# VectorE adds a tile to x before it makes the preceding tile's low part: the order of two loops in a two-layer encoder trunk

## The chip, the core and the metric

The kernel runs on one core of one Trainium2 chip. The metric is the device time of one execution in microseconds (us), the median of several runs. The engines are named as the profile names them: PE (TensorE, matrix products), PEld (its weight loads), DVE (VectorE), ACT (ScalarE), POOL (GpSimd) and SP (SyncE, which issues most transfers here).

## What is computed

Two layers of an encoder over 1088 tokens (1024 of a new stream, 64 of a running one) with 1024 channels; float32 throughout:

```python
hn = rmsnorm(x, g_mix)
proj = hn @ w_in
y_a, h_last = s5_mixer(u_a, ...)
y_b, new_hist = pool_mixer(u_b, ...)
x = x + jnp.concatenate([y_a, y_b], axis=-1) @ w_out
hf = rmsnorm(x, g_ffn)
x = x + jnp.square(jax.nn.relu(hf @ w_ff1)) @ w_ff2
```

`rmsnorm` divides by the root of the mean square over the channels and multiplies by a gain. After the second layer a last `rmsnorm` gives the output.

## The kernel before

x lies in SBUF with channels on the partitions, as `KD` = 8 tiles of 128 channels x 1088 tokens. Each product of float32 matrices is made of three products of fp32r parts: a number is split into a high part (a rounding copy, made by ACT) and a low part (the number minus the high part, made by DVE), and PE computes high x high, low x high and high x low. One output tile of 128 channels x 1088 tokens fills three banks of PSUM; there are two such tiles (`ps`), used in turn by the tile's number. A tile with `k` input tiles takes 9 `k` matmuls (three products, three column ranges): 36 in the products with four input tiles, 72 in those with eight.

The weights come in blocks of 128 x 1024 through two slots: SP fetches a block (`w_raw`), ACT makes its high part (`split_hi`, L861, tile `w_high`), DVE its low part (`split_lo`, L1223, tile `w_low`). A block serves two output tiles of four input tiles, or one of eight. SP fetches block b when the low part of block b-2 is made, since that frees the slot.

The stages of a layer, in order: `WIN` (u = normalised x times w_in), the two mixers with the first residual products (`WOB`), the gate (`GLU`), the **second residual products** (`WOA`: x += W_out y_a, 8 tiles of four input tiles), then the feed-forward in `NC` = 8 chunks. A chunk `cc` has `KA` = 4 tiles of the first matrix (`ff1_tile`, eight input tiles each) and 8 tiles of the second (`ff2_tile`, four input tiles each), which are added to x. After the last chunk of layer 0 comes layer 1's `WIN`. There the norm is begun as soon as x is final, tile by tile: the input of the next products is x times gain, in two parts, tiles `h_high` and `h_low`; the division by the root mean square is put on the result of those products later, once the sum of squares is known (`rms`).

Two loops over the 8 output tiles m thus end with making h: that of the second residual products in both layers, and that of the last chunk of layer 0's feed-forward. All engines work their own queue in the order in which the program was written; semaphores join them. For each tile m:

- PE computes tile m into `ps[m % 2]`. It waits in `tile_at` for `tile_free`, that is, until DVE has taken tile m-2 out of the same PSUM tile.
- DVE `add_to_x` (L1548, two instructions) adds the PSUM tile to x[m] and so frees it.
- ACT `finish` (L885, L887) then makes the square of x[m] (tiles `work_r` and `work_s` in turn, `rms` for m = 0) and `h_high`[m]; after an odd m, `ahead` makes the high part of the next weight block (L861). At the end of layer 0's feed-forward ACT also issues a transfer that keeps x[m] in DRAM.
- POOL `add_squares` (L1764) adds the square to `rms`.
- DVE, after an odd m, makes the low part of that weight block, `split_lo` (L1223).
- DVE `low_h` (L1227) waits for `h_high`[m] and makes `h_low`[m].

In `products` (L509 is the matmul) the first tile of the following stage takes its eight input tiles one after the other and waits before input tile k for `h_low`[k] (`h_made`). After that tile PE sums the squares over the channels (`sum_part`, L538), which waits for POOL's last addition; ACT takes the root (L895), DVE the reciprocal (`inverse`, L1239), and only then does DVE take the first output tile out of PSUM (L1682 or L1501).

Of the kernel before, what the change touches and what calls it, by code (L numbers as in the profile page):

```python
# [14 lines left out]
LAYERS = 2  # L15
# [7 lines left out]
KD = DM // P  # L23
# [10 lines left out]
B_WIN, B_WOB, B_GLU, B_WOA, B_FF = 0, 8, 12, 14, 18  # L34
FFC = DFF // P // KD
NC = 2 * FFC
# [15 lines left out]
L_FFN, L_NEXT, L_SCALE, NLP = 0, 8, 16, 20  # L52
# [62 lines left out]
def hybrid_trunk(nc, x_in, w_blocks, w_pool, prep_in, gain0, layer_in, dstate_in,  # L115
# [10 lines left out]
    with ExitStack() as ctx:  # L126
# [3 lines left out]
        def at(name, offset, shape, dt=F32):  # L130
            assert offset + int(np.prod(shape[1:])) <= words, name
            return nc.alloc_sbuf_tensor_at(name, list(shape), dt, offset=base + 4 * offset)
# [109 lines left out]
        lp = at("layer_params", S + 136, [P, NLP])  # L242
# [87 lines left out]
        def f32(ap):  # L330
            return ap.bitcast(F32)

        def halves(tile, flat, also=()):

            yield (tile[:, 0:2, 0:WIDE], flat[:, 0:2 * WIDE].rearrange("p (c n) -> p c n", c=2),
                   *(a[:, 0:2 * WIDE].rearrange("p (c n) -> p c n", c=2) for a in also))
            yield (tile[:, 2, 0:2 * J], flat[:, 2 * WIDE:T], *(a[:, 2 * WIDE:T] for a in also))
# [15 lines left out]
        def ff1_tile(l, cc, m):  # L353
            return l * NT + T_FF + 12 * cc + m

        def ff2_tile(l, cc, m):
            return l * NT + T_FF + 12 * cc + KA + m

        def ff_block(l, cc, n):

            return l * NB + B_FF + 8 * cc + n

        def w_parts(b):

            hi, lo = (whi_last, wlo_last) if b >= LAYERS * NB - 2 else (whi, wlo)
            return hi[:, b % 2, :], lo[:, b % 2, :]

        def last_tile(i):

            c, m = divmod(i, KD)  # L370
            a, b = CHUNKS[c]
            return c, m, slice(a * J, b * J), ps[i % 6 // 3][:, i % 3, 0:(b - a) * J]
# [832 lines left out]
        def _(v):  # L1205
# [13 lines left out]
            def split_lo(b):  # L1219
                if b < LAYERS * NB:  # L1220
                    v.wait_ge(whi_made, b + 1)
                    hi, lo = w_parts(b)
                    v.tensor_tensor(lo, raw[:, b % 2, :], f32(hi), ALU.subtract).then_inc(wlo_made, 1)  # L1223

            def low_h(m, n, gain):
                v.wait_ge(hhi_made, n + 1)
                v.scalar_tensor_tensor(hlo[:, m, :], x[:, m, :], gain[:, m:m + 1], f32(hhi[:, m, :]),  # L1227
                                       ALU.mult, ALU.subtract).then_inc(h_made, 1)
# [99 lines left out]
            def rotations(l, piece, tmp=None):  # L1328
                d = prep_of[l]
                tmp = d.rot_tmp if tmp is None else tmp  # L1330
                if piece == 0:
                    first_rotations(step, copy, tt, l, (1, 2, 4, 8), tmp)
                elif piece == 1:
                    if l == 0:
                        v.wait_ge(first_rot, 1)
                    for n in (16, 32):
                        doubled(step, tt, l, n, slice(0, 2), tmp)
                else:
                    h = piece - 2
                    doubled(step, tt, l, 64, h, tmp)  # L1340
                    step.wait()
                    for i in range(2):
                        ins = v.tensor_copy(d.rot[:, h, i, :, JP:J], d.rot[:, h, i, :, 0:JS])
                        if i:
                            ins.then_inc(rot_made, 1)
                        else:
                            step(ins)
# [144 lines left out]
            for l in range(LAYERS):  # L1492
                LB, LT = l * NB, l * NT
# [51 lines left out]
                def add_to_x(n, m):  # L1545
                    v.wait_ge(tile_done, n + 1)
                    for pt_, xt in halves(ps[n % 2], x[:, m, :]):
                        ins = v.tensor_tensor(xt, pt_, xt, ALU.add)  # L1548
                    ins.then_inc(tile_free, 1)
# [119 lines left out]
                    v.tensor_tensor(yal[:, m, :], ya[:, m, :], f32(yah[:, m, :]), ALU.subtract).then_inc(ya_made, 1)  # L1669
                for m in range(KD):  # L1670
                    add_to_x(LT + T_WOA + m, m)
                    if m % 2:
                        split_lo(LB + B_WOA + m // 2 + 2)
                    low_h(m, l * 16 + 8 + m, lp[:, L_FFN:L_FFN + KD])

                inverse(2 * l + 1)
                for cc in range(NC):
                    for m in range(KA):
                        n = ff1_tile(l, cc, m)
                        v.wait_ge(tile_done, n + 1)  # L1680
                        for pt_, out, r in halves(ps[n % 2], tr[:, :], (rms[:, :],)):
                            ins = v.scalar_tensor_tensor(out, pt_, 0.0, r, ALU.max, ALU.mult)  # L1682
                        ins.then_inc(tile_free, 1)
                        v.wait_ge(tile_free, n + 1 + 2)
                        v.tensor_tensor(ts[:, :], tr[:, :], tr[:, :], ALU.mult).then_inc(sq_v, 1)  # L1685
                        split_lo(ff_block(l, cc, m) + 2)
                        h = (l * NC + cc) * KA + m + 1
                        v.wait_ge(sq_v, h)
                        v.wait_ge(ghi_made, h)
                        v.tensor_tensor(glo[:, m, :], ts[:, :], f32(ghi[:, m, :]), ALU.subtract).then_inc(hid_made, 1)  # L1690
                        if l == 0:
                            if cc == 1 and m == 0:
                                angles(1)
                            elif cc == 1 and m == 1:
                                discretised(1)
                            elif cc == 2 and m < 2:
                                rotations(1, 1 + m)
                            elif cc in PREP_CHUNKS:
                                if m == 1:
                                    drive_weights(1, PREP_CHUNKS[cc])  # L1700
                                if m == 2:
                                    carry_weights(1, PREP_CHUNKS[cc])
                    if l == LAYERS - 1 and cc == NC - 1:
                        break
                    for m in range(KD):
                        n = ff2_tile(l, cc, m)
                        add_to_x(n, m)
                        if m % 2:
                            split_lo(ff_block(l, cc, KA + m // 2) + 2)
                        if l == 0 and cc == 1 and m == 2:  # L1710
                            rotations(1, 0)
                        if l == 0 and cc == 2 and m == 2:
                            rotations(1, 3)
                        if cc == NC - 1 and l + 1 < LAYERS:
                            low_h(m, l * 16 + 16 + m, lp[:, L_NEXT:L_NEXT + KD])

            def last_inverse(c):
                a, b = CHUNKS[c]
# [21 lines left out]
            for i in range(3 * KD):  # L1740
                c, m, cols, out = last_tile(i)
# [248 lines left out]
```

## Time and profile before

| | |
|---|---|
| runs shown | 2132.12, 2132.76, 2133.49 us; median 2132.76 us |
| span of the profiled execution | 2130.4 us, from its first to its last instruction |
| that execution's own time | only its span is recorded; the median of the runs lies 2.4 us above it |
| PE, PEld, DVE, ACT, POOL busy | 2068.2, 2032.8, 1079.0, 447.0, 212.2 us |
| share of PE in the chain that ended last | 87% |
| granted PE clock, mean | 0.994 |

Times in the trace are microseconds from the start of the span. In a timeline row stand the start, the time from the first start to the last end of what is merged in it, the engine, the line, the operation, what it writes and reads, and in brackets the idle time before it with what ended that. Three matmuls, one for each column range, are merged in a row of PE; the length of such a row holds the last matmul's passage through the array, so the pace of PE is read from the starts of following rows. In the second residual products of layer 0 PE works from 248.2 us on, in those of layer 1 from 1297.1 us on; the eight tiles at the end of layer 0's feed-forward start at 1024.75 us.

### The profile page before, as it was taken

The page shows a single profiled execution, that of the slowest core. Times are in us where ns is not written, and L with a number is a line of the kernel's source. Part 1 is how long each engine was busy: PE and PEld are TensorE (multiplying, and loading weights), DVE is VectorE, ACT ScalarE, POOL GpSimd, SP SyncE. Part 2 cuts the span into 40 slices and gives each one's busy share as a digit, 9 for nine tenths or more (in the row PEclk, how much of TensorE's full clock was granted, in tenths as well). Part 3 has the DMA queues.
Part 4 walks back from the last instruction along what each step waited for, and adds up shares of the span by engine and source line. Part 5 has one row for each costly group of instructions (what it writes and reads, how often), then busy time and mean ns, then how long its engine had stood idle before and what let it go on. Part 6 is the DMA issues. An engine that isn't in the chain of part 4 may idle for free.

```text
span 2130.4 us, 29080 instructions
## 1 busy us (share of the span) xinstructions
PE 2068.2 (97%) x12888; PEld 2032.8 (95%) x12888; DVE 1079.0 (51%) x1423; ACT 447.0 (21%) x560; POOL 212.2 (10%) x294
## 2 busy tenths in 40 slices
PE   8999899999999999999999999999999999999997
PEld 7888899999999999999999889999999999999997
DVE  7988464455453535353558725643333434343346
ACT  6232431211011111111332234311110101111112
POOL 2253120000000000010110331100000000000002
PEclk9999999999999999999999999999999999999999
DMA  4555111111211112123232641111111111111112
GB/s 172 139 147 165 50 55 50 40 50 40 92 60 51 60 42 70 42 71 122 92 124 80 183 121 38 47 42 48 40 50 40 50 40 50 40 49 41 43 47 84
DMA packets 62493, 152.77 MB, mean 72 GB/s; under 512 B 8576, under 2 KB 21408, under 8 KB 61984
## 3 DMA queue, kind: packets, MB, share of 16 engines
q1 hardware_dynamic: 49552, 112.76, 16.8%
q0 software_dynamic: 9072, 24.65, 4.1%
q10 hardware_dynamic: 3744, 13.50, 1.6%
q8 instruction: 101, 1.65, 0.3%
q14 instruction: 24, 0.20, 0.0%
HBM read 123.36 MB, written 27.53 MB: 71 GB/s over the span
## 4 chain that ended last, share of the span: by engine, by line
PE 87%; DVE 6%; ACT 3%; issue 2%; DMA 1%; POOL 0%; ACTq 0%; DVEq 0%; POOLq 0%
PE tile L509 82%; DVE h_low L1227 2%; PE tile L827 2%; DVE x L1548 1%; ACT h_high L887 1%; DVE w_low L1223 1%; ACT w_high L861 1%; PE small L721 1%; PE small L715 1%; PE small L623 1%; PE small L597 0%; DVE pool_s L1210 0%; POOL y_a L1835 0%; DMA ya_dram<-u_blocks 0%; DMA y_a<-ya_dram 0%
## 5 line engine op out<-in xcount | busy, mean ns | idle before, releaser
L509 PE MATMUL tile<-h_high,w_high 128*128 128x408 f32 (+1 forms) x1920 | 426.9, 330 | 17.1 <-DVE w_low L1223 10.6
L1548 DVE TENSOR_TENSOR x<-tile,x 128x816 f32<-128x816 f32 (+1 forms) x304 | 205.4, 717 | 455.3 <-PE tile L509 445.2
L509 PE MATMUL tile<-h_high,w_low 128*128 128x408 f32 (+1 forms) x1920 | 423.1, 328 | 0.0
L509 PE MATMUL tile<-h_low,w_high 128*128 128x408 f32 (+1 forms) x1920 | 422.8, 328 | 0.0
L509 PEld LDWEIGHTS tile<-h_high,w_high 128*128 128x128 f32 x1920 | 320.9, 188 | 22.0 <-issue 13.5
L509 PEld LDWEIGHTS tile<-h_high,w_low 128*128 128x128 f32 x1920 | 320.4, 188 | 1.1
L509 PEld LDWEIGHTS tile<-h_low,w_high 128*128 128x128 f32 x1920 | 320.2, 188 | 1.0
L509 PE MATMUL tile<-hidden_high,w_high 128*128 128x408 f32 (+1 forms) x1440 | 318.3, 329 | 2.1 <-DVE x L1548 1.2
L509 PE MATMUL tile<-hidden_low,w_high 128*128 128x408 f32 (+1 forms) x1440 | 316.4, 328 | 0.0
L509 PE MATMUL tile<-hidden_high,w_low 128*128 128x408 f32 (+1 forms) x1440 | 316.3, 328 | 0.0
L861 ACT ACTIVATE w_high<-w_raw 128x1024 fp32r<-128x1024 f32 x162 | 170.5, 1052 | 661.4 <-PE tile L509 653.9
L1682 DVE SCALAR_TENSOR_TENSOR work_r<-tile,rms 128x816 f32<-128x816 f32 (+1 forms) x128 | 86.7, 718 | 357.9 <-PE tile L509 357.7
L1223 DVE TENSOR_TENSOR w_low<-w_raw,w_high 128x1024 fp32r<-128x1024 f32 x162 | 202.5, 1250 | 91.5 <-ACT w_high L861 91.3
L509 PEld LDWEIGHTS tile<-hidden_high,w_high 128*128 128x128 f32 x1440 | 239.2, 188 | 8.3 <-issue 7.2
L509 PEld LDWEIGHTS tile<-hidden_high,w_low 128*128 128x128 f32 x1440 | 239.6, 188 | 0.7
L509 PEld LDWEIGHTS tile<-hidden_low,w_high 128*128 128x128 f32 x1440 | 239.6, 188 | 0.7
L1161 ACT ACTIVATE hidden_high<-work_r 128x1088 fp32r<-128x1088 f32 x64 | 71.4, 1116 | 636.5 <-DVE work_r L1682 636.5
L1685 DVE TENSOR_TENSOR work_s<-work_r 128x1088 f32<-128x1088 f32 x64 | 82.7, 1292 | 2.2
L1690 DVE TENSOR_TENSOR hidden_low<-work_s,hidden_high 128x1088 fp32r<-128x1088 f32 x64 | 82.2, 1284 | 0.0
L1900 POOL TENSOR_TENSOR rms<-rms,work_s 128x408 f32<-128x408 f32 x8 | 9.3, 1160 | 730.5 <-ACT work_s L1196 730.0
L1227 DVE SCALAR_TENSOR_TENSOR h_low<-x,layer_params,h_high 128x1088 fp32r<-128x1088 f32 x24 | 43.9, 1830 | 27.3 <-ACT h_high L887 27.3
L1764 POOL TENSOR_TENSOR rms<-rms,work_s 128x1088 f32<-128x1088 f32 x12 | 30.6, 2546 | 206.4 <-ACT work_s L885 206.4
(212 smaller groups left out, 1694.0 us busy)
## 6 DMA issues: line engine op xcount, KB each, us to landing
w_raw<-w_blocks SPq DMA_DIRECT2D x164, 512.0 KB, 3.5
x<-x_t ACTq DMA_DIRECT2D x8, 544.0 KB, 10.8
u_blocks<-ua_dram SPq DMA_DIRECT2D x64, 68.0 KB, 2.7
ya_dram<-u_blocks ACTq DMA_DIRECT2D x8, 544.0 KB, 3.2
y_a<-ya_dram POOLq DMA_DIRECT2D x64, 68.0 KB, 2.7
x_kept<-x ACTq DMA_DIRECT2D x8, 544.0 KB, 2.7
cy_dram<-y_quarter POOLq DMA_DIRECT2D x16, 256.0 KB, 2.9
carry_weights<-cy_dram POOLq DMA_DIRECT2D x8, 512.0 KB, 5.6
```

The lines of the kernel that those rows point to most:

```text
L509: mm = pe.matmul(ps[tile][:, c, 0:(b - a) * J], lhs, xt[:, k, a * J:b * J], start=(first and n == 0), stop=(last and n == 2))
L623: mm = pe.matmul(out[:, k * 2 * P:(k + 1) * 2 * P], wp[:, 2 * half + k, :], folded(raw[:, b % 2, :], half)[:, k], start=True, stop=True)
L827: mm = pe.matmul(out, wt[:, lhs], xt[:, k, cols], start=(k == 0 and n == 0), stop=(k == KA - 1 and n == 2))
L861: act.activation(w_parts(b)[0], raw[:, b % 2, :], ACT.Copy).then_inc(whi_made, 1)
L1161: act.activation(ghi[:, m, :], tr[:, :], ACT.Square).then_inc(ghi_made, 1)
L1223: v.tensor_tensor(lo, raw[:, b % 2, :], f32(hi), ALU.subtract).then_inc(wlo_made, 1)
L1227: v.scalar_tensor_tensor(hlo[:, m, :], x[:, m, :], gain[:, m:m + 1], f32(hhi[:, m, :]), ALU.mult, ALU.subtract).then_inc(h_made, 1)
L1548: ins = v.tensor_tensor(xt, pt_, xt, ALU.add)
L1682: ins = v.scalar_tensor_tensor(out, pt_, 0.0, r, ALU.max, ALU.mult)
L1685: v.tensor_tensor(ts[:, :], tr[:, :], tr[:, :], ALU.mult).then_inc(sq_v, 1)
L1690: v.tensor_tensor(glo[:, m, :], ts[:, :], f32(ghi[:, m, :]), ALU.subtract).then_inc(hid_made, 1)
L1764: pool.tensor_tensor(rms[:, :], rms[:, :], (tr, ts)[m % 2][:, :], ALU.add).then_inc(sq_added, 1)
```

## The change

In both loops the low part of h moves behind the addition of the following tile. In the second residual products the order for tile m becomes: add tile m to x; make `h_low`[m-1]; after an odd m other than the last, the weight block's low part. After the loop come `h_low`[7] and the low part of the last block. In the last chunk of layer 0's feed-forward (`turning`) the order is the same, with `h_low`[6], `h_low`[7] and the weight block's low part behind the last addition. No instruction is added or taken away, and the queues of PE, ACT, POOL and SP are the same.

```diff
                 for m in range(KD):
                     add_to_x(LT + T_WOA + m, m)
-                    if m % 2:
+                    if m:
+                        low_h(m - 1, l * 16 + 8 + m - 1, lp[:, L_FFN:L_FFN + KD])
+                    if m % 2 and m < KD - 1:
                         split_lo(LB + B_WOA + m // 2 + 2)
-                    low_h(m, l * 16 + 8 + m, lp[:, L_FFN:L_FFN + KD])
+                low_h(KD - 1, l * 16 + 8 + KD - 1, lp[:, L_FFN:L_FFN + KD])
+                split_lo(LB + B_WOA + KD // 2 - 1 + 2)
...
+                    turning = cc == NC - 1 and l + 1 < LAYERS
                     for m in range(KD):
                         n = ff2_tile(l, cc, m)
                         add_to_x(n, m)
+                        if turning and m:
+                            low_h(m - 1, l * 16 + 16 + m - 1, lp[:, L_NEXT:L_NEXT + KD])
+                        if turning and m == KD - 1:
+                            low_h(m, l * 16 + 16 + m, lp[:, L_NEXT:L_NEXT + KD])
                         if m % 2:
                             split_lo(ff_block(l, cc, KA + m // 2) + 2)
...
-                        if cc == NC - 1 and l + 1 < LAYERS:
-                            low_h(m, l * 16 + 16 + m, lp[:, L_NEXT:L_NEXT + KD])
```

DVE's queue in the middle of layer 0's second residual products, from the addition of tile 2 to that of tile 4, before (x is the residual stream, `tile` the PSUM tile, `w_low` the low part of a weight block):

```order
L1548 TENSOR_TENSOR x<-tile,x 128x816
L1548 TENSOR_TENSOR x<-tile,x 128x272
L1227 SCALAR_TENSOR_TENSOR h_low<-x,layer_params,h_high 128x1088
L1548 TENSOR_TENSOR x<-tile,x 128x816
L1548 TENSOR_TENSOR x<-tile,x 128x272
L1223 TENSOR_TENSOR w_low<-w_raw,w_high 128x1024
L1227 SCALAR_TENSOR_TENSOR h_low<-x,layer_params,h_high 128x1088
L1548 TENSOR_TENSOR x<-tile,x 128x816
L1548 TENSOR_TENSOR x<-tile,x 128x272
```

The same place in the changed kernel:

```order
L1548 TENSOR_TENSOR x<-tile,x 128x816
L1548 TENSOR_TENSOR x<-tile,x 128x272
L1227 SCALAR_TENSOR_TENSOR h_low<-x,layer_params,h_high 128x1088
L1548 TENSOR_TENSOR x<-tile,x 128x816
L1548 TENSOR_TENSOR x<-tile,x 128x272
L1227 SCALAR_TENSOR_TENSOR h_low<-x,layer_params,h_high 128x1088
L1223 TENSOR_TENSOR w_low<-w_raw,w_high 128x1024
L1548 TENSOR_TENSOR x<-tile,x 128x816
L1548 TENSOR_TENSOR x<-tile,x 128x272
```

The rows read alike, but the low part now belongs to the tile before: behind the addition of tile 2 stands `h_low`[1], behind that of tile 3 `h_low`[2], and the weight block's low part comes after it instead of before. DVE's queue at the end of the same loop, from the addition of tile 6 to the reciprocals, in the changed kernel:

```order
L1548 TENSOR_TENSOR x<-tile,x 128x816
L1548 TENSOR_TENSOR x<-tile,x 128x272
L1227 SCALAR_TENSOR_TENSOR h_low<-x,layer_params,h_high 128x1088
L1548 TENSOR_TENSOR x<-tile,x 128x816
L1548 TENSOR_TENSOR x<-tile,x 128x272
L1227 SCALAR_TENSOR_TENSOR h_low<-x,layer_params,h_high 128x1088 x2
L1223 TENSOR_TENSOR w_low<-w_raw,w_high 128x1024
L1239 RECIPROCAL rms<-rms 128x408 x2
L1239 RECIPROCAL rms<-rms 128x272
```

Before, the end read: addition of tile 7, `w_low`, one `h_low`, reciprocals. Now two low parts of h stand behind the last addition, and the weight block's low part is last ahead of the reciprocals.

## Rows read from the trace of the kernel before

**Rows 1.** Page, part 1: busy us (share of span) and instructions.

```profile
PE 2068.2 (97%) x12888; PEld 2032.8 (95%) x12888; DVE 1079.0 (51%) x1423; ACT 447.0 (21%) x560; POOL 212.2 (10%) x294
```

**Rows 2.** Two stretches: busy us (count) by engine, PEclk, DMA share, GB/s.

```profile
253.41:311.00 57.59, 55.72 (x333) 55.02 (x334) 31.18 (x28) 22.75 (x21) 17.82 (x7) 1.00 0.17 58
...
1036.89:1091.00 54.11, 49.98 (x294) 48.43 (x295) 29.70 (x26) 22.06 (x21) 17.80 (x7) 1.00 0.34 123
```

**Rows 3.** Waits of PE, 1030 to 1110 us: total, times, longest.

```profile
PE tile L509 <- DVE x L1548: 2.4, 2, 1.2
PE tile L509 <- DVE h_low L1227: 1.6, 1, 1.6
```

**Rows 4.** PE's timeline, layer 0, second residual products; start, length.

```profile
254.00 0.66 PE L509 MATMUL tile<-y_a_low,w_high 128*128 128x408 f32 x3
...
296.22 0.66 PE L509 MATMUL tile<-y_a_high,w_low 128*128 128x408 f32 x3
...
297.15 0.73 PE L509 MATMUL tile<-h_high,w_high 128*128 128x408 f32 x3 [0.27 <-issue]
...
309.41 0.76 PE L509 MATMUL tile<-h_high,w_high 128*128 128x408 f32 x3 [1.60 <-DVE h_low L1227]
...
310.01 0.66 PE L509 MATMUL tile<-h_low,w_high 128*128 128x408 f32 x3
```

**Rows 5.** Timeline of PE, layer 1, second residual products.

```profile
1302.91 0.66 PE L509 MATMUL tile<-y_a_low,w_high 128*128 128x408 f32 x3
...
1358.31 0.76 PE L509 MATMUL tile<-h_high,w_high 128*128 128x408 f32 x3 [1.58 <-DVE h_low L1227]
```

**Rows 6.** Timeline of PE, end of layer 0's feed-forward.

```profile
1037.46 0.66 PE L509 MATMUL tile<-hidden_low,w_high 128*128 128x408 f32 x3
...
1062.74 0.74 PE L509 MATMUL tile<-hidden_high,w_high 128*128 128x408 f32 x3 [1.25 <-DVE x L1548]
...
1076.21 0.76 PE L509 MATMUL tile<-h_high,w_high 128*128 128x408 f32 x3 [1.16 <-DVE x L1548]
...
1088.50 0.76 PE L509 MATMUL tile<-h_high,w_high 128*128 128x408 f32 x3 [1.59 <-DVE h_low L1227]
```

**Rows 7.** Chain of work, in order of time: start us, us, count.

```profile
360.72 95.60 PE tile L509 x576
```

**Rows 8.** Timeline of DVE, layer 0, second residual products.

```profile
268.57 1.34 DVE L1548 TENSOR_TENSOR x<-tile,x 128x816 f32<-128x816 f32 x2
272.19 2.66 DVE L1227 SCALAR_TENSOR_TENSOR h_low<-x,layer_params,h_high 128x1088 fp32r<-128x1088 f32 x1 [2.28 <-ACT h_high L887]
274.77 1.34 DVE L1548 TENSOR_TENSOR x<-tile,x 128x816 f32<-128x816 f32 x2
279.34 1.62 DVE L1223 TENSOR_TENSOR w_low<-w_raw,w_high 128x1024 fp32r<-128x1024 f32 x1 [3.22 <-ACT w_high L861]
280.88 1.34 DVE L1227 SCALAR_TENSOR_TENSOR h_low<-x,layer_params,h_high 128x1088 fp32r<-128x1088 f32 x1
282.14 1.34 DVE L1548 TENSOR_TENSOR x<-tile,x 128x816 f32<-128x816 f32 x2
...
301.89 1.34 DVE L1548 TENSOR_TENSOR x<-tile,x 128x816 f32<-128x816 f32 x2
...
308.01 1.34 DVE L1227 SCALAR_TENSOR_TENSOR h_low<-x,layer_params,h_high 128x1088 fp32r<-128x1088 f32 x1
```

**Rows 9.** Timeline of ACT, same stretch, the odd tile at 274.77.

```profile
276.14 1.11 ACT L885 ACTIVATE work_s<-x 128x1088 f32<-128x1088 f32 x1 [3.99 <-DVE x L1548]
277.16 1.19 ACT L887 ACTIVATE h_high<-x,layer_params 128x1088 fp32r<-128x1088 f32 x1
278.26 1.04 ACT L861 ACTIVATE w_high<-w_raw 128x1024 fp32r<-128x1024 f32 x1
```

**Rows 10.** Timeline of POOL, same stretch, one addition of squares.

```profile
271.15 2.55 POOL L1764 TENSOR_TENSOR rms<-rms,work_r 128x1088 f32<-128x1088 f32 x1 [4.84 <-ACT work_r L885]
```

**Rows 11.** Timeline of DVE, end of layer 0's feed-forward, addition of tile 1.

```profile
1040.29 1.35 DVE L1548 TENSOR_TENSOR x<-tile,x 128x816 f32<-128x816 f32 x2
```

## The prediction

> **What bounds the kernel now.** I read the page's part 1 first: PE is busy for 97% of the span, DVE for 51% [rows 1]. A change of order on DVE can only gain where PE still waits for DVE, so I looked up PE's waits in the two kinds of stretch that the change touches. There the granted clock is 1.00, so the rows are at full clock throughout, and PE is busy for 55.7 of 57.6 us in the one and 50.0 of 54.1 us in the other [rows 2]. At the end of layer 0's feed-forward PE waits twice for an addition to x (2.4 us) and once for a low part of h (1.6 us) [rows 3]. Idle times are counted from the modelled end of the last matmul, so they are short of the whole loss; that is worked out below from starts.
>
> DVE's rows tell why. Additions of even tiles start at 268.57 and 282.14, so two tiles take DVE 13.57 us [rows 8]. Little of that is work: 2.28 us it waits for `h_high` of the even tile and 3.22 us for `w_high` behind the odd one, each time right after its own addition [rows 8], because ACT can begin the square only when the addition is done and needs 1.11, 1.19 and 1.04 us for its instructions [rows 9]. The low part of the even tile also takes 2.66 us where that of the odd takes 1.34 [rows 8]: it falls on POOL's addition of squares (271.15 to 273.70 us [rows 10]).
>
> PE's own pace for two tiles: a row of three matmuls follows the other every (296.22 - 254.00) / 85 = 0.497 us [rows 4], a tile has 12 such rows, two tiles 11.92 us. So DVE falls behind by 1.65 us a pair. In the second residual products it starts early enough that PE notices only at the end: a break at 297.15, then 1.60 us before the last input tile, at 309.41, where `h_low`[7] is late [rows 4]; its row starts at 308.01 and lasts 1.34 us [rows 8]. Layer 1 shows the same wait at 1358.31 [rows 5]. At the end of layer 0's feed-forward tiles 0 and 1 finish almost together, so DVE is a tile behind from the start, and PE waits at 1062.74, 1076.21 and 1088.50 [rows 6].
>
> **The change, part by part.** Nothing is added or taken away; DVE's instructions in these loops change places, and no other queue does. What is moved is `h_low`[m], past the addition of tile m+1, and past `split_lo` where one stands there.
>
> *The pair of tiles.* From the start of an odd tile's addition: 1.34 us addition, then `h_low` of the tile before, whose `h_high` has been ready for long, so no wait: 1.34 us [rows 8]. ACT meanwhile makes square, `h_high` and `w_high`, and DVE still waits for `w_high`, which comes 3.22 us after the addition [rows 8]; so `h_low` costs nothing there, its cover is that wait, and without the cover it would cost 1.34 us. Then 1.62 us for `w_low`: 1.34 + 3.22 + 1.62 = 6.2 us. The even tile: 1.34 + 1.34 = 2.7 us, or 4.0 if its low part falls on POOL (2.66). Together 8.9 to 10.2 us, where PE needs 11.92: DVE is ahead, and PE sets the pace.
>
> By the Trainium skill, "SBUF — State Buffer", section "Who interferes with whom", a VectorE instruction with two SBUF inputs and a GpSimd one that reads SBUF exclude each other for a whole instruction, and the one that came first holds the port; the 2.66 us agree with that [rows 8, 10]. By that rule the moved low part, which comes before POOL's addition, takes 1.34 and not 2.66 us; by either the pair stays under PE's.
>
> *Second residual products, layer 0.* From 254.00 to the last input tile of the first feed-forward tile are 107 rows of PE: 2 left in tile 0, 84 of tiles 1 to 7 and 21 of input tiles 0 to 6. Without a break it starts at 254.00 + 107 x 0.497 = 307.15; it started at 309.41. The first row after a break is 0.10 us longer (310.01 - 309.41 = 0.60) [rows 4]. Gain 2.26 + 0.10 = 2.36 us, if `h_low`[7] is there by 307.15. It is: tile 7 ends near 296.9, addition to 298.2, `h_high`[7] at 300.5 (2.28 us later), and `h_low`[7], behind `h_low`[6], ends at 301.9, or 303.2 beside POOL. 3.9 us to spare.
>
> *Second residual products, layer 1.* The same: 1302.91 + 53.15 = 1356.06 against 1358.31 [rows 5], with the restart 2.35 us.
>
> *End of layer 0's feed-forward.* From 1037.46 to the last input tile of layer 1's first tile are 71 rows to the end of tile 7 and 21 more: 92 x 0.497 = 45.70, so 1083.16 against 1088.50 [rows 6]; with the restart 5.44 us. Does DVE catch up? The addition of tile 1, at 1040.29 before [rows 11], can now start when that tile ends, near 1036.9. It ends at 1038.2; ACT, busy with tile 0 until 1039.0, needs 1.11 + 1.19 + 1.04 us more [rows 9] and gives `w_high` at about 1042.3; `w_low` to 1043.9; addition of tile 2 to 1045.3. Tile 4 needs that at 1037.46 + 23 x 0.497 = 1048.9: 3.6 us to spare, and from there the pair's account holds.
>
> *What is late next.* `split_lo` now stands behind the low part. For m = 1, 3 and 5 its block is wanted by the tile m+3, 11.92 us after tile m; it is there after 6.2. The last one stands behind both low parts: 303.2 + 1.62 = 304.8 in layer 0, against about 308.0 before, when it ended just ahead of `h_low`[7] (308.01 [rows 8]), so the fetch behind it starts earlier than now. PE wants this block at 308.6. POOL's last addition begins once the square of tile 7 is made, near 299.4, and ends near 302 [rows 10], so the sum over channels after the first tile (308.6) waits for nothing new. What follows, roots and reciprocals, starts from PE's sums and moves up with them. I cost all this at nothing; the cover is those 3.8 to 6 us.
>
> **The sum.** 2.36 + 2.35 + 5.44 = 10.15 us. This takes the stage's pace; over a long run without breaks PE needs 95.60 / 576 x 3 = 0.498 us a row [rows 7], by which the gain is 9.8. From below, PE's counted waits alone (2.4 + 1.6 [rows 3], 1.60 + 0.27 [rows 4], 1.58 [rows 5]) give 7.45. I take 10.0, since starts measure the loss whole: 2130.4 - 10.0 = 2120.4 us of span. The runs' median lies 2.4 us above the span of the profile, so the time is 2122.8 us. What a measurement can tell from no change is about 0.2%, 4.3 us: from 2128.5 to 2137.0.
>
> **The rivals.**
> - *Only part comes* (11%). One kind of stretch keeps a wait: then either the feed-forward's end alone gains, 2132.8 - 5.4 = 2127.4, or the two residual stages alone, 2132.8 - 4.7 = 2128.1. For it: at the feed-forward's end DVE and ACT start a tile late, and ACT also issues transfers there. Against: 3.6 us to spare at the narrowest place.
> - *PE is full, the order of DVE is worth nothing* (6%): 2132 to 2133 us. For it: 97% busy, and DVE, at 51%, is not the bound [rows 1]. Against: the waits end with DVE's rows by name [rows 3], and starts leave 10 us. It would hold if what follows waited for something that does not move up, as a transfer; I find none. The Trainium skill, "Perfetto Trace Analysis", section "Identifying the Most-Contended Engine", says to optimise the engine with the highest occupancy first, for TensorE by the busy share of its weight loads; by that (95%) this is a change on the wrong engine. The same page's "Optimization Strategy" looks at the gaps of that engine, and those are what the rows show.
> - *The last weight block comes too late* (3%): slower. `split_lo` of the last block is now behind two low parts of h, and the first low part behind ACT's work on tile 7. PE's second tile of the next stage stands still until it is made, at a price of 1 us for 1 us at three places. It decides when it ends later than 308.6, that is 3.8 us after my 304.8; no gain is left when it ends 7.1 us after, and 10 us after give 3 x (10 - 3.8) - 10 = 8.6 us more: 2141. Against: all of DVE's and ACT's rows in question sum to less.
>
> **How the numbers follow.** Forecast 80%, its own range 2121.5 (the sum of 10.15 on the runs' lowest, 2132.12, is 2122.0, less 0.5 for pace) to 2125.5 (7.45 on the median is 2125.3). Partial gain 11%, nothing 6%, slower 3%. To hold 8 of 10 and most of the partial cases the range goes up to 2127.5, and down to 2121, for one small break more that closes elsewhere. Faster by over 0.2%: the forecast and nearly all of the partial case, 0.90. Within: 0.07. Slower: 0.03.
>
> **What would show it.** In PE's timeline of the changed kernel the breaks that end with an addition to x or with `h_low` are gone in all three stretches; the last input tile's row follows 1.49 us after that before it; DVE waits for PE before most additions instead of falling behind, and no longer for `h_high` except for tile 7. `h_low` takes 1.34 us nearly everywhere. I am wrong if PE waits there for `w_low`, for a landing of `w_raw`, or if the stretches are shorter by some 10 us and a later stretch longer.

## The result and the profile after

The changed kernel takes 2121.39 us (median of 4 runs, 2119.67 to 2122.81) against 2132.79 us before; the ratio is 0.9950, with a 95% interval from 0.9938 to 0.9962. The forecast was 2122.8 us. The profiled execution has a span of 2119.1 us, 11.3 less than that of before.

The busy times hardly change [rows 1]:

```profile
PE 2063.7 (97%) x12888; PEld 2030.9 (96%) x12888; DVE 1070.9 (51%) x1423; ACT 447.7 (21%) x560; POOL 214.1 (10%) x294
```

DVE does the same 1423 instructions in 8 us less (1079.0 before). The gain is in PE's waits, although PE's busy time falls too, by 4.5 us: the profile counts a part of each break as busy. To see where, each of the three stretches is measured from its first matmul to the first sum over channels (L538) behind it, in PE's timeline (start, length, engine, line; in brackets idle time and what ended it). Before:

```profile
248.22 0.66 PE L509 MATMUL tile<-y_a_high,w_high 128*128 128x408 f32 x3
...
311.00 1.19 PE L538 MATMUL small<-rms,ones 128*128 128x408 f32 x3
...
1024.75 0.66 PE L509 MATMUL tile<-hidden_high,w_high 128*128 128x408 f32 x3
...
1091.58 1.53 PE L538 MATMUL small<-rms,ones 128*128 128x408 f32 x4
...
1297.11 0.66 PE L509 MATMUL tile<-y_a_high,w_high 128*128 128x408 f32 x3
...
1359.91 1.53 PE L538 MATMUL small<-rms,ones 128*128 128x408 f32 x4
```

After, with the first rows of the feed-forward's or layer 1's first tile (295.23, 1068.86) and the last input tile's row of the first stretch (305.65):

```profile
246.72 0.66 PE L509 MATMUL tile<-y_a_high,w_high 128*128 128x408 f32 x3
...
295.23 0.65 PE L509 MATMUL tile<-h_high,w_high 128*128 128x408 f32 x3
...
305.65 0.66 PE L509 MATMUL tile<-h_high,w_high 128*128 128x408 f32 x3
...
307.15 1.19 PE L538 MATMUL small<-rms,ones 128*128 128x408 f32 x3
...
1020.89 0.66 PE L509 MATMUL tile<-hidden_high,w_high 128*128 128x408 f32 x3
...
1068.86 0.65 PE L509 MATMUL tile<-h_high,w_high 128*128 128x408 f32 x3
...
1082.27 1.53 PE L538 MATMUL small<-rms,ones 128*128 128x408 f32 x4
...
1288.35 0.66 PE L509 MATMUL tile<-y_a_high,w_high 128*128 128x408 f32 x3
...
1348.78 1.53 PE L538 MATMUL small<-rms,ones 128*128 128x408 f32 x4
```

| stretch | before, us | after, us | gain | forecast |
|---|---|---|---|---|
| second residual products, layer 0 | 62.78 | 60.43 | 2.35 | 2.36 |
| end of layer 0's feed-forward | 66.83 | 61.38 | 5.45 | 5.44 |
| second residual products, layer 1 | 62.80 | 60.43 | 2.37 | 2.35 |
| sum | 192.41 | 182.24 | 10.17 | 10.15 |

Each length is the difference of two starts in the fences. None of these rows after has idle time in brackets, where before the last input tile's rows waited 1.58 to 1.60 us for `h_low` and two rows at the feed-forward's end for the addition [rows 4, 5, 6]. At the feed-forward's end PE is now busy for 61.33 of 61.38 us; before, it was for 62.65 of 66.83. Over all three stretches its counted idle time falls from 9.0 to 1.2 us, which is 7.8 of the 10.17 gained.

```profile
1020.89:1082.27 61.38, 61.33 (x372) 60.89 (x371) 33.41 (x33) 24.71 (x24) 17.97 (x7) 1.00 0.34 123
```

DVE's timeline in layer 0's second residual products, an even and an odd tile in the middle and the end of the loop, answers to [rows 8]:

```profile
265.81 1.34 DVE L1548 TENSOR_TENSOR x<-tile,x 128x816 f32<-128x816 f32 x2
...
271.59 1.35 DVE L1548 TENSOR_TENSOR x<-tile,x 128x816 f32<-128x816 f32 x2 [3.18 <-PE tile L509]
272.86 1.35 DVE L1227 SCALAR_TENSOR_TENSOR h_low<-x,layer_params,h_high 128x1088 fp32r<-128x1088 f32 x1
276.17 1.63 DVE L1223 TENSOR_TENSOR w_low<-w_raw,w_high 128x1024 fp32r<-128x1024 f32 x1 [1.97 <-ACT w_high L861]
277.73 1.34 DVE L1548 TENSOR_TENSOR x<-tile,x 128x816 f32<-128x816 f32 x2
278.99 1.34 DVE L1227 SCALAR_TENSOR_TENSOR h_low<-x,layer_params,h_high 128x1088 fp32r<-128x1088 f32 x1
...
295.43 1.35 DVE L1548 TENSOR_TENSOR x<-tile,x 128x816 f32<-128x816 f32 x2 [3.17 <-PE tile L509]
...
299.06 2.64 DVE L1227 SCALAR_TENSOR_TENSOR h_low<-x,layer_params,h_high 128x1088 fp32r<-128x1088 f32 x1 [1.02 <-ACT h_high L887]
301.63 1.21 DVE L1223 TENSOR_TENSOR w_low<-w_raw,w_high 128x1024 fp32r<-128x1024 f32 x1
```

The additions of even tiles start 11.92 us apart (265.81, 277.73), which is PE's pace; before it was 13.57. DVE waits 3.18 us for PE's tile, so it has time to spare. The low part of h starts right behind an addition and needs no wait except for tile 7. At the feed-forward's end that of tile 0 waits as well, 0.79 us for `h_high`, since the additions of tiles 0 and 1 follow each other there at once. All but one of each loop take the short time, as the group of the 24 low parts shows (lowest, median and highest duration in ns):

```profile
L1227 DVE SCALAR_TENSOR_TENSOR h_low<-x,layer_params,h_high x24: 1337/1344/2650, 260.9 to 1340.7; 128x1088 fp32r<-128x1088 f32 x24
```

The rest of the 11.3 us is not from the change. PE's first row of the second residual products of layer 0 starts 1.50 us earlier than before (246.72 against 248.22), and up to there the programs are the same. In the profiles of the experiments below this start lies between 246.93 and 250.21 us, in no order that fits their edits.

Much of this difference is PE's granted clock. Between 35 and 45 us PE works without a break in both executions, but the clock is 0.83 on average before and 1.00 after; rows there follow at 0.90 us (38.35, 39.26, 40.16) where they follow at 0.50 at full clock, so it was at the lower of its two levels for a while. From the row of L547 to that of L555 PE takes 11.06 us before (34.51 to 45.57) and 9.51 after (35.12 to 44.63), 1.55 us apart. The changed kernel in e5 (below) has the slow form, 11.04 us, and so has e4; the other experiments have the clock at 1.00 there, among them e3 and e7 with the old order. So it goes with the execution and not with the change. What sets it off was not tried. A second difference lies between the stretches: from the sum behind the feed-forward's end to layer 1's residual products it takes 206.08 us after and 205.53 before, and 203.86 to 205.93 in the experiments. The gain is therefore read from the stretches.

### The profile page after: what moved, and what is told of

It is laid out like the page before. It is cut to its first block, busy times and chain, and to the rows that moved or that the text cites. A ratio compares the mean times of both kernels' runs of the same rounds, so it can differ in the third digit from the quotient of the medians.

```text
span 2119.1 us, 29080 instructions
## 1 busy us (share of the span) xinstructions
PE 2063.7 (97%) x12888; PEld 2030.9 (96%) x12888; DVE 1070.9 (51%) x1423; ACT 447.7 (21%) x560; POOL 214.1 (10%) x294
## 3 DMA queue, kind: packets, MB, share of 16 engines
q8 instruction: 101, 1.65, 0.3%
## 4 chain that ended last, share of the span: by engine, by line
PE 94%; DVE 2%; ACT 2%; issue 1%; DMA 1%; POOL 0%; ACTq 0%; DVEq 0%; POOLq 0%
PE tile L509 89%; PE tile L827 2%; PE small L721 1%; PE small L715 1%; PE small L623 1%; PE small L597 0%; ACT w_high L861 0%; DMA y_a<-ya_dram 0%; DVE pool_s L1210 0%; POOL y_a L1841 0%; DMA ya_dram<-u_blocks 0%; PE small L565 0%; PE small L538 0%; DVE y_a L1665 0%; ACT u_blocks L1095 0%
## 5 line engine op out<-in xcount | busy, mean ns | idle before, releaser
L509 PE MATMUL tile<-pooled_high,w_high 128*128 128x408 f32 (+1 forms) x192 | 44.2, 338 | 4.4 <-DVE pooled_low L1542 4.2
```

Of the source, the lines that this page charges most:

```text
L509: mm = pe.matmul(ps[tile][:, c, 0:(b - a) * J], lhs, xt[:, k, a * J:b * J], start=(first and n == 0), stop=(last and n == 2))
```

## The experiments

The theory: PE waited because DVE needed 13.57 us for two tiles and PE 11.92; any way to bring DVE under 11.92 gives the gain, and each stretch gains by itself. Rivals: only the order matters and not the pace; the collision with POOL's addition is all of it; the difference lies elsewhere.

**One part alone (e1, e2).** In e1 only the residual loop has the new order: the kernel before with the first part of the change's diff, the loop of the second residual products. In e2 only the last chunk of layer 0's feed-forward has it: the changed kernel with that part taken back.

> Only the second residual products of both layers have the new order; the end of layer 0's feed-forward has the old one. Theory (VectorE's pace of 13.57 us for two tiles against TensorE's 11.92 is what made TensorE wait, and each stretch gains by itself): 2.36 + 2.35 = 4.7 us less than before, about 2128.1 us; TensorE's breaks are gone in the two residual stretches and unchanged (5.4 us) at the feed-forward's end. Rival (the stretches depend on each other, or the gain is a difference from execution to execution in the first 250 us): no fixed share, or 0 to 1.5 us.

> Only the end of layer 0's feed-forward has the new order. Theory: 5.4 us less than before, about 2127.4 us, and the two waits for the last low part (1.6 us in the idle times, 2.36 us in the starts) stay in the residual stretches. The gains of this run and of the one with the residual products alone sum to 10.1 us. Rival: the parts sum to clearly more or less.

Measured: 2127.56 us with the residual part alone, ratio 0.9977 (0.9967 to 0.9986); 2126.68 us with the feed-forward's end alone, 0.9973 (0.9962 to 0.9983); before 2132.63 us beside them. The stretches, measured as above, are 60.41, 66.84 and 60.42 us in e1 and 62.80, 61.37 and 62.78 in e2: each has the length of after where it was changed, of before where it was not. Two of the waits left in e1, in PE's timeline at the feed-forward's end:

```profile
1059.18 0.73 PE L509 MATMUL tile<-hidden_high,w_high 128*128 128x408 f32 x3 [1.25 <-DVE x L1548]
...
1084.96 0.76 PE L509 MATMUL tile<-h_high,w_high 128*128 128x408 f32 x3 [1.60 <-DVE h_low L1227]
```

and in e2, at the ends of the two residual stretches:

```profile
309.63 0.77 PE L509 MATMUL tile<-h_high,w_high 128*128 128x408 f32 x3 [1.59 <-DVE h_low L1227]
...
1352.14 0.76 PE L509 MATMUL tile<-h_high,w_high 128*128 128x408 f32 x3 [1.60 <-DVE h_low L1227]
```

These are the waits of before, to two hundredths. The parts' gains by the medians (5.1 and 6.0 us) sum to 11.0, by the stretches to 4.7 + 5.5 = 10.2. The stretches do not depend on each other, and the rival of a fixed difference elsewhere falls.

**The collision taken away, order of before (e3).** In `add_squares` POOL leaves out the addition for every even tile and only gives its signal, so the sums of squares lack those tiles:

```diff
-                    pool.tensor_tensor(rms[:, :], rms[:, :], (tr, ts)[m % 2][:, :], ALU.add).then_inc(sq_added, 1)
+                    if m % 2:
+                        pool.tensor_tensor(rms[:, :], rms[:, :], (tr, ts)[m % 2][:, :], ALU.add).then_inc(sq_added, 1)
+                    else:
+                        pool.sem_inc(sq_added, 1)
```

> The order of before; GpSimd leaves out the additions of the squares of tiles 2, 4 and 6 in all sums of squares over whole tiles (the norms are wrong by that). This takes away what makes the low part of an even tile last 2.66 us. Theory: that low part falls to 1.34 us, two tiles take VectorE 13.57 - 1.30 = 12.27 us, still over TensorE's 11.92; the residual stretches lose their whole wait (the last low part ends 3.9 us earlier), the feed-forward's end keeps about 1.5 of 5.4 us: about 8.6 us less than before, 2124.2 us. Rival A (the wait for ScalarE in VectorE's queue is the whole cause, the collision with GpSimd costs nothing): 2132.8 us. Rival B (the collision is the whole cause): 2122.7 us, no break left anywhere.

Measured: 2123.67 us, 0.9958 (0.9944 to 0.9971). DVE's timeline, an even tile, and the even tile's addition after that:

```profile
268.99 1.34 DVE L1548 TENSOR_TENSOR x<-tile,x 128x816 f32<-128x816 f32 x2
272.61 1.35 DVE L1227 SCALAR_TENSOR_TENSOR h_low<-x,layer_params,h_high 128x1088 fp32r<-128x1088 f32 x1 [2.28 <-ACT h_high L887]
...
281.27 1.34 DVE L1548 TENSOR_TENSOR x<-tile,x 128x816 f32<-128x816 f32 x2
```

The even low part takes 1.35 us where it took 2.66, and two tiles 12.28 us (281.27 - 268.99). The residual stretches are as short as in the changed kernel (60.43 and 60.42 us), the feed-forward's end takes 62.98, 1.6 us more than there. That is the theory's middle case in each number. Rival A falls; Rival B falls too, though only by the feed-forward's end. With 12.28 us DVE still falls behind PE's 11.92, by 0.36 us a pair: too little to reach PE before a residual loop is over, and in keeping with the 1.6 us left where DVE starts a tile late.

The new order also does a second thing, at the loop's end: `h_low`[7] no longer stands behind `w_low`. e3 shows that the residual stretches do not need that, since it has the old end and loses nothing there. What that swap would give by itself was not run. An estimate from the trace of before: `h_high`[7] is ready at 305.47 and POOL's addition runs from 304.46 to 307.01, so `h_low`[7] would end near 308.1 (1.1 us behind POOL, as in the row of 2.66) instead of 309.35, which is about half of a residual stretch's gain; at the feed-forward's end the two waits for an addition would stay.

**ScalarE makes the high part first, order of before (e4).** In `finish` the two activations change places.

```diff
+                if gain is not None:
+                    act.activation(hhi[:, m, :], x[:, m, :], ACT.Copy, scale=gain[:, m:m + 1]).then_inc(hhi_made, 1)
                 if m > 2:
                     act.wait_ge(sq_added, 7 * (phase - 1) + m - 2)
                 dst = (tr, ts)[m % 2] if m else rms
                 act.activation(dst[:, :], x[:, m, :], ACT.Square).then_inc(sq_made, 1)
-                if gain is not None:
-                    act.activation(hhi[:, m, :], x[:, m, :], ACT.Copy, scale=gain[:, m:m + 1]).then_inc(hhi_made, 1)
```

> The order of before on VectorE; ScalarE makes the high part of h first and the square after it, so the wait of an even low part falls by 1.1 us and GpSimd's addition comes after that low part. Theory: even tile 1.28 + 1.2 + 1.34 = 3.9 us; odd tile 1.28 + wait for the weight's high part; there GpSimd's addition now begins 1.1 us later and holds the weight's low part up until it ends, 8.4 us in all; pair 12.3 us, about 8.5 us less than before, 2124.3 us. Rival (GpSimd's addition does not hold up the weight's low part): odd tile 7.4 us, pair 11.3 us, about 10 us less, 2122.8 us. Second rival (only VectorE's order counts, not its pace): 2132.8 us.

Measured: 2124.51 us, 0.9962 (0.9950 to 0.9975). DVE's timeline, one pair:

```profile
271.62 1.34 DVE L1548 TENSOR_TENSOR x<-tile,x 128x816 f32<-128x816 f32 x2
274.23 1.35 DVE L1227 SCALAR_TENSOR_TENSOR h_low<-x,layer_params,h_high 128x1088 fp32r<-128x1088 f32 x1 [1.27 <-ACT h_high L883]
275.50 1.35 DVE L1548 TENSOR_TENSOR x<-tile,x 128x816 f32<-128x816 f32 x2
280.07 2.72 DVE L1223 TENSOR_TENSOR w_low<-w_raw,w_high 128x1024 fp32r<-128x1024 f32 x1 [3.22 <-ACT w_high L861]
282.71 1.34 DVE L1227 SCALAR_TENSOR_TENSOR h_low<-x,layer_params,h_high 128x1088 fp32r<-128x1088 f32 x1
283.97 1.34 DVE L1548 TENSOR_TENSOR x<-tile,x 128x816 f32<-128x816 f32 x2
```

and POOL's additions beside it:

```profile
275.28 2.71 POOL L1764 TENSOR_TENSOR rms<-rms,work_r 128x1088 f32<-128x1088 f32 x1 [5.93 <-ACT work_r L887]
279.17 2.54 POOL L1764 TENSOR_TENSOR rms<-rms,work_s 128x1088 f32<-128x1088 f32 x1 [1.18 <-ACT work_s L887]
```

The pair takes 12.35 us. The even low part waits 1.27 us and not 2.28, and is over before POOL can hold it up; instead POOL's addition at 275.28, begun while that low part still ran, takes 2.71 us and not 2.54, and the weight's low part, which comes 0.9 us into the next addition (279.17 to 281.71), takes 2.72 us. By that row and by the pair the first rival falls (no hold-up, a pair of 11.3 us); the medians alone would not tell it from the theory. What the edit saves on the even tile it partly gives back on the odd one. Stretches 60.41, 63.30, 60.44: again the gain goes with DVE's pace, and not with its order alone. Here, too, the pace stays above 11.92 us, and 1.9 us are left at the feed-forward's end. That a pace under 11.92 leaves no break is shown by the changed order (8.7 us of work in a pair, below), not by e3 or e4.

**Starting a tile late (e5, e6, e7).** PE interleaves tiles 0 and 1 of the second residual products, as it does in the feed-forward, in the changed kernel (e6) and in that of before (e7):

```diff
-                for n in range(KD):
-                    half_tile(B_WOA, T_WOA, n, yah, yal, None if n else lambda k: pe.wait_ge(ya_made, l * KA + k + 1))
+                block_at(LB + B_WOA)
+                for n in range(2):
+                    tile_at(LT + T_WOA + n)
+                    for k in range(KA - 1):
+                        if n == 0:
+                            pe.wait_ge(ya_made, l * KA + k + 1)
+                        products(n, 0, KA * n + k, k, yah, yal, k == 0, False)
+                pe.wait_ge(ya_made, l * KA + KA)
+                for n in range(2):
+                    products(n, 0, KA * n + KA - 1, KA - 1, yah, yal, False, True).then_inc(tile_done, 1)
+                for n in range(2, KD):
+                    half_tile(B_WOA, T_WOA, n, yah, yal)
```

The changed kernel ran once more beside them (e5).

> The changed kernel once more, as the measure for the others of this set. Theory: 10.2 us of its gain are the change (2.36 + 5.45 + 2.38 us in the three stretches of the profile shown), the rest is a difference between executions in the first 250 us: in this profile the three stretches have the same lengths to 0.1 us, and the time from the start to the second residual products of layer 0 differs by up to 2 us. Rival (the change does something ahead of its first place, too): that time is again 1.5 us below the one of before.

> The changed kernel, and TensorE interleaves tiles 0 and 1 of the second residual products as it does elsewhere: input tiles 0 to 2 of both tiles, then input tile 3 of both, so that it need not wait for the last low part of y_a. Theory: the break of 0.72 us and its restart of 0.10 us ahead of that input tile go in both layers, 1.65 us less than the changed kernel; VectorE now begins a tile late there too, but with 8.9 to 10.2 us for a pair it catches up, so no new break. Rival (VectorE is as near to the edge as at the feed-forward's end before): 2 to 3 us lost in each of the two stretches, so about 3 us more than the changed kernel.

> The same interleaving of tiles 0 and 1 with VectorE's order of before. Theory (what makes the feed-forward's end lose 5.4 us and the residual stretches 2.4 is only that VectorE begins a tile late there): each residual stretch now loses about 5.4 us, less the 0.8 us gained: 2 x (5.4 - 2.4 - 0.8) = 4.5 us slower than before, 2137.2 us. Rival (the difference between the stretches has another cause, as the transfers that keep x): no more than 1.6 us faster than before, 2131.1 us.

The changed kernel again: 2122.58 us, 0.9953 (0.9940 to 0.9965), before 2132.26. Its stretches are 60.42, 61.38 and 60.44 us, in sum 182.24 as in the first profile, while its start of the second residual products is at 249.87, later than the 248.22 of before. So the change is worth 10.2 us, and the 1.5 us more of the first profile were that execution's.

With the order of before the interleaving costs: 2136.05 us, 1.0020 (1.0011 to 1.0029). The residual stretches grow from 62.8 to 65.38 and 65.31 us, 2.6 and 2.5 more where 2.2 to 2.3 was forecast; the rival, by which this kernel is up to 1.6 us faster than before, falls. They show the waits that only the feed-forward's end had, in PE's timeline of the first (the second stands as "issue", but starts 0.10 us after the end of an addition, 297.13 + 1.34 us):

```profile
285.03 0.73 PE L509 MATMUL tile<-y_a_high,w_high 128*128 128x408 f32 x3 [1.24 <-DVE x L1558]
...
298.57 0.74 PE L509 MATMUL tile<-h_high,w_high 128*128 128x408 f32 x3 [1.23 <-issue]
...
310.82 0.77 PE L509 MATMUL tile<-h_high,w_high 128*128 128x408 f32 x3 [1.57 <-DVE h_low L1237]
```

With this start a residual stretch takes 65.38 us in the old order and 59.88 in the new (e6, below), a difference of 5.5. So the interleaved start accounts for the 5.4 us of the feed-forward's end against 2.4 elsewhere.

With the changed order it gains: 2118.83 us, 0.9940 (0.9928 to 0.9953). By the medians it is 3.8 us under the changed kernel beside it, but the intervals of the two overlap; the stretches show the difference, 59.88 and 59.90 us for 60.43, together 1.1 us. It is less than the 1.65 forecast, since one small break came new, in front of tile 2 (0.71 us from the row before, where rows follow at 0.50, and the next one at 0.57):

```profile
259.16 0.73 PE L509 MATMUL tile<-y_a_high,w_high 128*128 128x408 f32 x3
```

That row cannot start before tile 0 is taken out of PSUM, and tile 0 now ends only 1.5 us before tile 1. This is the fastest kernel of the study by its median.

**Loading DVE again (e8).** In the changed kernel each of the 24 low parts is made twice, with the same result:

```diff
             def low_h(m, n, gain):
                 v.wait_ge(hhi_made, n + 1)
+                if n >= KD:
+                    step(v.scalar_tensor_tensor(hlo[:, m, :], x[:, m, :], gain[:, m:m + 1], f32(hhi[:, m, :]),
+                                                ALU.mult, ALU.subtract))
+                    step.wait()
                 v.scalar_tensor_tensor(hlo[:, m, :], x[:, m, :], gain[:, m:m + 1], f32(hhi[:, m, :]),
                                        ALU.mult, ALU.subtract).then_inc(h_made, 1)
```

> The changed kernel, with every low part of h behind the residual products and at the feed-forward's end made twice (the second overwrites the first with the same numbers), to load VectorE by 1.4 us a tile. Theory (VectorE has slack, and a low part that meets GpSimd's addition stands until that ends): the second low part meets the addition in every tile, two tiles take VectorE 13.7 us, it falls behind by 1.8 us a pair, and the stretches lose 4.4, 7.5 and 4.4 us: about 16 us slower than the changed kernel, 2137 us. Rival (only the instructions' own lengths count): 10.3 us a pair, no break, the time of the changed kernel, 2121.4 us.

Measured: 2133.93 us, 1.0009 against before (1.0000 to 1.0018), 11.4 us more than the changed kernel beside it. DVE's timeline, an even tile and the next even tile's addition:

```profile
267.22 1.34 DVE L1552 TENSOR_TENSOR x<-tile,x 128x816 f32<-128x816 f32 x2
268.49 1.34 DVE L1228 SCALAR_TENSOR_TENSOR h_low<-x,layer_params,h_high 128x1088 fp32r<-128x1088 f32 x1
269.86 3.63 DVE L1231 SCALAR_TENSOR_TENSOR h_low<-x,layer_params,h_high 128x1088 fp32r<-128x1088 f32 x1
273.41 1.34 DVE L1552 TENSOR_TENSOR x<-tile,x 128x816 f32<-128x816 f32 x2
...
280.74 1.34 DVE L1552 TENSOR_TENSOR x<-tile,x 128x816 f32<-128x816 f32 x2
```

POOL's addition beside it:

```profile
269.80 2.54 POOL L1774 TENSOR_TENSOR rms<-rms,work_r 128x1088 f32<-128x1088 f32 x1 [4.78 <-ACT work_r L885]
```

The first low part (L1228) takes 1.34 us; the second (L1231) starts 0.06 us after POOL's addition and takes 3.63, until 1.15 us after that has ended. Two tiles take 13.52 us (13.7 forecast), and PE waits again, at the last two input tiles of the first feed-forward tile:

```profile
306.72 0.77 PE L509 MATMUL tile<-h_high,w_high 128*128 128x408 f32 x3 [1.86 <-DVE h_low L1231]
...
309.37 0.77 PE L509 MATMUL tile<-h_high,w_high 128*128 128x408 f32 x3 [0.89 <-DVE h_low L1231]
```

The rival, by which only the instructions' own lengths count, falls. The size was off: 16 us forecast, 11.4 measured. The stretches lose 3.6, 4.1 and 4.9 us where 4.4, 7.5 and 4.4 were forecast (1.3 of the 4.9 have another cause, in the last section); the 7.5 carried the ratio of before over to an order in which the addition of tile 1 no longer stands behind a low part, which may be why it is too high; that was not tested.

## Why the prediction was right

- **What bounds it.** "DVE falls behind by 1.65 us a pair" was the reason, and taking 1.30 us of that away by another means, with the order untouched (e3), gave most of the gain, while loading DVE to 13.52 us a pair with the new order gave it all back (e8).
- **The pair.** Forecast 8.9 to 10.2 us of DVE's time under PE's 11.92. Measured: the odd tile's addition to the end of `w_low` 6.2 us (271.59 to 277.80), as forecast; addition and low part of the even tile 2.6 us (277.73 to 280.33 with the low part of 1.34 us at 278.99), so 8.7 in all (271.59 to 280.33). That is a little under the forecast's lower end, since following rows overlap by up to 0.1 us. The cover of the moved low part is as named: `w_high` comes 3.31 us after the low part's start, 1.34 of it is now work and 1.97 wait.
- **The three stretches.** 2.36, 5.44 and 2.35 us forecast, 2.35, 5.45 and 2.37 measured. Counting rows from a start and comparing with the start that was, with the longer first row after a break, was the right measure: the idle times alone gave 7.45. The narrowest place, the catching up at the feed-forward's end, came out as worked out, too: the addition of tile 2 was to end at 1045.3 and ends at 1041.27, in a stretch that starts 3.86 us earlier, so 0.2 us ahead of the forecast.
- **The choice of 10.0 between 9.8 and 10.15.** The upper end was right: the stretch's own pace holds, and that of the long run without breaks has no bearing here.
- **The end of the loop.** With the start 1.5 us earlier, the forecast ends for `h_low`[7] and the last `w_low` are 301.7 and 303.3; measured are 301.70 and 302.84. The last low part meets POOL's addition (2.64 us), as the later of the two bounds had it. `w_low` takes 1.21 us, since POOL's addition (298.01 to 300.55) is over by then. The 1.62 of the forecast, taken from the middle of the loop, holds a wait for POOL: after the change, `w_low` at 276.17 takes 1.63 us beside an addition from 274.18 to 276.72.
- **The shared port.** That an instruction of DVE with two operands in SBUF stands until POOL's addition ends was taken from [rows 8, 10] and from the Trainium skill, "SBUF — State Buffer", section "Who interferes with whom". e8 shows it sharply (3.63 us = the rest of POOL's 2.54 and 1.15 more), e4 from the other place in the queue (`w_low` 2.72 behind POOL). That POOL waits for DVE in turn rests on 0.17 us in one row (2.71 for 2.54) and is weak. The trace agrees with the page in that the addition to x, with one operand in PSUM, is not slowed: 1.35 us at 275.50 in e4, beside POOL.
- **The rivals.** No part stayed out (partial gain). What follows did move up: from the sum behind the first stretch to the first row of the next, 713.7 us before and after (1024.75 - 311.00 and 1020.89 - 307.15). The last weight block was not late. That PE is full and the order of DVE worth nothing did not hold: PE's busy share is 97% before and after, and 10 us went out of the three stretches. The Trainium skill, "Perfetto Trace Analysis", section "Identifying the Most-Contended Engine", says to optimise the engine with the highest occupancy first, and the time was in that engine's gaps; the prediction's words "a change on the wrong engine" took it too narrowly.

What the prediction did not have is that the time up to 250 us differs by 3.5 us between executions, in part with the granted clock; the range's lower end, 2121.0, was argued otherwise, and that it held the median of 2121.39 is luck. The second set (e5) gave 2122.58 us, 9.7 us under the kernel before, nearer to the forecast of 10.0.

## What to carry to other kernels

On an engine that works its queue in order, do not put an instruction that needs another engine's answer right behind the one that the other engine answers to; put the next tile's independent work between them, and see that what is delayed by it has a wait to hide in. Judge it by the time that a period takes the engine against the period of the engine that it feeds, and count the loss from starts over the whole stretch and not from idle times. An order with slack also lets other steps be rearranged: interleaving two tiles cost 5.1 us in the two residual stretches with the old order and gained 1.1 with the new.

## What the runs showed of the hardware beyond that

In e8 the granted clock of PE fell to 0.50, the lower of its two levels (1.2 GHz), at the end of layer 1's residual stretch, and was back in the stretch from 1364 us on. Before it, PE had waited 1.86 us for a low part of h, worked for 1.85 us, and waited 0.80 us for the next (PE's timeline, layer 1):

```profile
1355.63 0.76 PE L509 MATMUL tile<-h_high,w_high 128*128 128x408 f32 x3 [1.86 <-DVE h_low L1231]
...
1358.28 1.28 PE L509 MATMUL tile<-h_high,w_high 128*128 128x408 f32 x3 [0.80 <-DVE h_low L1231]
```

In layer 0 two like waits (1.86 and 0.89 us, with 1.76 us of work between them) left the clock at 1.00. The rows by stretch (busy us and count of PE, PEld, DVE, ACT, POOL, then PEclk, DMA share, GB/s):

```profile
309.00:311.00 2.00, 1.63 (x10) 1.63 (x11) 1.45 (x2) 0.00 (x0) 0.00 (x0) 1.00 0.00 0
1350.00:1355.00 5.00, 3.77 (x23) 3.48 (x22) 4.96 (x4) 4.28 (x4) 2.53 (x1) 1.00 0.00 0
1358.00:1361.00 3.00, 2.72 (x9) 2.69 (x10) 1.36 (x2) 0.00 (x0) 0.00 (x0) 0.50 0.25 41
1364.00:1368.00 4.00, 4.00 (x25) 3.91 (x24) 4.00 (x2) 1.03 (x2) 0.00 (x0) 1.00 0.00 0
```

The stretch is 1.3 us longer than that of layer 0 (65.34 against 64.04), which is the cost of the fall up to the sum over channels: its last three rows take 2.88 us instead of 1.60. Counted on to the same row behind it (1358.28 to 1367.17 against 309.37 to 315.57, 8.89 against 6.20 us) the cost is 2.7 us. So after two short waits close together the clock fell in one place and not in the other; what tells the two apart was not tried. It was not part of the gain: in the three stretches of the change the granted clock is 1.00 in both kernels.
